# Sparse attention on one Trainium2 core: the masks move from TensorE to the maximum, the step pipeline gets one stage longer, and one weight load moves ahead of the parameters

## The reference

```
score = einsum(iw, relu(iq . ik)); causal keys only; idx = top_k(score, 128)
logits = q . k_sel * dh ** -0.5        # 8 heads of 128, 2 key/value heads
logits = where(valid, logits, -inf)
p = softmax(logits); o = p . v_sel
```

## Time and profile before

| | |
|---|---|
| median of 3 runs | 2177.53 us (2177.52 to 2177.66) |
| profiled execution | 2177.74 us |
| its span, first to last instruction | 2176.0 us |
| PE busy | 2135.4 us, 98% |
| DVE busy | 1285.1 us, 59% |
| ACT busy | 917.7 us, 42% |
| chain that ended last | PE 88%, DVE 5%, ACT 5% |
| the sparse attention (logits of step 0 to the first matmul of the next stage) | 1396.04 to 1467.43 us |

### The profile page before, as it was taken

How to read it: one execution, slowest core, us unless ns; L and a number is a source line. 1 busy time by engine, 2 the same in 40 slices (tenths; PEclk the granted TensorE clock), 3 DMA queues, 4 the chain that set the end, 5 groups by cost and what they waited for, 6 DMA issues and landing times.

```text
span 2176.0 us, 26697 instructions
## 1 busy us (share of the span) xinstructions
PE 2135.4 (98%) x10620; PEld 1730.3 (80%) x10620; DVE 1285.1 (59%) x1966; ACT 917.7 (42%) x1550; POOL 101.5 (5%) x155
## 2 busy tenths in 40 slices
PE   9999999999999999999999999999999999999998
PEld 7866688888888658888888878777788878888887
DVE  6446475555347767655543749456677657555634
ACT  4235553334325456333432642344445545333421
POOL 0000040000000003100000000000012200000000
PEclk9999999999999999999999999999999999999999
DMA  5312123333323203333332323202222023333332
GB/s 201 97 59 78 60 96 97 97 97 116 97 78 107 68 30 126 97 97 97 116 97 88 126 78 90 75 30 87 79 77 68 2 78 98 97 97 98 117 97 77
DMA packets 51099, 194.00 MB, mean 89 GB/s; under 512 B 5665, under 2 KB 5665, under 8 KB 49953
## 3 DMA queue, kind: packets, MB, share of 16 engines
q1 hardware_dynamic: 50976, 192.30, 28.1%
HBM read 188.09 MB, written 4.19 MB: 88 GB/s over the span
## 4 chain that ended last, share of the span: by engine, by line
PE 88%; DVE 5%; ACT 5%; issue 1%; DMA 1%; SPq 0%; ACTq 0%; DVEq 0%
PE bank L403 26%; PE bank L404 26%; PE bank L405 26%; PE bank L980 2%; PE bank L703 1%; DMA ring<-stream 1%; ACT arena L1265 1%; PE bank L681 1%; DVE small L1889 1%; ACT whi L1160 1%; PE bank L618 1%; DVE arena L2010 0%; DVE xs L1884 0%; PE bank L692 0%; PE bank L775 0%
## 5 line engine op out<-in xcount | busy, mean ns | idle before, releaser
L403 PE MATMUL bank<-xs,whi 128*128 128x512 f32 (+2 forms) x1992 | 770.8, 387 | 8.4 <-DVE xs L1884 2.9
L405 PE MATMUL bank<-xs,wlo 128*128 128x512 f32 (+2 forms) x1992 | 750.1, 377 | 0.0
L404 PE MATMUL bank<-xs,whi 128*128 128x512 f32 (+2 forms) x1992 | 749.9, 376 | 0.0
L1863 DVE TENSOR_TENSOR wlo<-ring,whi 128x1024 fp32r<-128x1024 f32 x333 | 415.2, 1248 | 294.8 <-ACT whi L1160 294.3
L1160 ACT ACTIVATE whi<-ring 128x1024 fp32r<-128x1024 f32 x333 | 350.4, 1054 | 262.4 <-DMA ring<-stream 262.2
L403 PEld LDWEIGHTS bank<-xs,whi 128*128 128x128 f32 x1992 | 375.4, 188 | 93.4 <-issue 12.2
L405 PEld LDWEIGHTS bank<-xs,wlo 128*128 128x128 f32 x1992 | 375.2, 188 | 69.0
L404 PEld LDWEIGHTS bank<-xs,whi 128*128 128x128 f32 x1992 | 375.8, 189 | 67.2 <-issue 2.9
L403 PE MATMUL bank<-whi,xs 128*128 128x512 f32 (+1 forms) x808 | 314.8, 390 | 1.6 <-issue 0.9
L405 PE MATMUL bank<-whi,xs 128*128 128x512 f32 (+1 forms) x808 | 311.7, 386 | 0.0
L404 PE MATMUL bank<-wlo,xs 128*128 128x512 f32 (+1 forms) x808 | 311.6, 386 | 0.0
(11 more groups left out here) (367 smaller groups left out, 1781.3 us busy)
## 6 DMA issues: line engine op xcount, KB each, us to landing
ring<-stream SPq DMA_DIRECT2D x333, 512.0 KB, 3.6
arena<-gains SPq DMA_DIRECT2D x5, 1024.0 KB, 5.8
arena<-xt SPq DMA_DIRECT2D x4, 512.0 KB, 6.1
arena<-xn SPq DMA_DIRECT2D x1, 2048.0 KB, 8.0
kept<-arena SPq DMA_DIRECT2D x1, 2048.0 KB, 7.2
arena<-kept SPq DMA_DIRECT2D x1, 2048.0 KB, 8.0
out<-arena SPq DMA_DIRECT2D x3, 512.0 KB, 2.6
con<-consts SPq DMA_DIRECT2D x1, 744.0 KB, 11.6
```

Source lines behind the costliest of these rows:

```text
L403: nc.tensor.matmul(out, ah, bh, start=first, stop=False)
L404: nc.tensor.matmul(out, ah, bl, start=False, stop=False)
L405: return nc.tensor.matmul(out, al, bh, start=False, stop=last)
L1863: V.tensor_tensor(wlo[:, v % SLOTS, :], ring[:, v % SLOTS, :], whi[:, v % SLOTS, :], ALU.subtract).then_inc(wlo_done, 1)
```

## The change

1. The mask matmuls on PE (line 683) are gone. DVE's maximum becomes one instruction that adds the mask to the logits, writes the negated sum back to the bank, and takes the minimum, which is the negated maximum; the minimum is read out by a second instruction. ACT's exponential gets scale -1. The wait for the masks moves from PE to DVE.
2. The pipeline is one step longer: after the logits of step n come the transposes of step n - 3 and the pv of step n - 4. ACT copies the transposed probabilities of step n - 3 ahead of the exponential of step n.
3. The three weight splits inside the stage are made at steps 5, 13 and 21 instead of 1, 9 and 17.
4. SP issues unit 1 ahead of the parameters.

The diff has the parts of SyncE, of the steps, of TensorE, of ScalarE and of VectorE in this order; the edit from `x == 1` to `x == 5` stands for ScalarE and for VectorE alike.

```diff
             for q in range(4):
                 sp.dma_start(U[:, 2 * q:2 * q + 2, :], xt[:, 2 * q:2 * q + 2, :]).then_inc(x_sem[q], 16)
+            sp.dma_start(ring[:, 1, :], stream[1]).then_inc(ring_sem[1], 16)
             sp.dma_start(par[:], params).then_inc(par_sem, 16)
-            for s in (1, 2, 3):
+            for s in (2, 3):
...
-                          more=[(idb[:], madd[:, i, 0:(i + 1) * P] if i else mqb[:], 0, (i + 1) * P)],
+                          mask=madd[:, i, 0:(i + 1) * P] if i else mqb[:],
...
-                for n in range(N + 3):
+                for n in range(N + 4):
...
-                        if n == 1:
-                            pe.wait_ge(vector_out, vector_at.find("masks"))
-                        nc.tensor.matmul(bank[b][:, 0:W], st["q"], st["k"], start=True, stop=False)
-                        for x, (l, r, c0, c1) in enumerate(st["more"]):
-                            m = nc.tensor.matmul(bank[b][:, c0:c1], l, r, start=False, stop=x == len(st["more"]) - 1)
-                        m.then_inc(tensor_out, tensor_at.next(name, "logits", n))
+                        nc.tensor.matmul(bank[b][:, 0:W], st["q"], st["k"], start=True, stop=True).then_inc(tensor_out, tensor_at.next(name, "logits", n))
...
-                    if 2 <= n < N + 2:
-                        k, st = n - 2, steps[n - 2]
+                    if 3 <= n < N + 3:
+                        k, st = n - 3, steps[n - 3]
...
-                    if n >= 3:
-                        k, st = n - 3, steps[n - 3]
+                    if n >= 4:
+                        k, st = n - 4, steps[n - 4]
...
+                    if 3 <= n < N + 3:
+                        k, st = n - 3, steps[n - 3]
+                        act.wait_ge(tensor_out, tensor_at.find(name, "t", k))
+                        if k >= 3:
+                            act.wait_ge(tensor_out, tensor_at.find(name, "pv", k - 3))
+                        A(st["ts"][:, 0:st["w"]], bank[5 + k % 2][:, 0:st["w"]], ACT.Copy).then_inc(scalar_out, scalar_at.next(name, "pt", k))
                     if n < N:
...
-                        A(st["ps"][:, 0:W], bank[st["lb"]][:, 0:W], ACT.Exp, bias=small[:, 200 + n % 4:201 + n % 4],
+                        A(st["ps"][:, 0:W], bank[st["lb"]][:, 0:W], ACT.Exp, bias=small[:, 200 + n % 4:201 + n % 4], scale=-1.0,
...
-                    if 2 <= n < N + 2:
-                        k, st = n - 2, steps[n - 2]
...
-                    if x == 1 and j < COUNT["z2b"]:
+                    if x == 5 and j < COUNT["z2b"]:
...
-                for n in range(N + 4):
+                for n in range(N + 5):
...
-                        V.tensor_reduce(small[:, 200 + n % 4:201 + n % 4], bank[steps[n]["lb"]][:, 0:steps[n]["w"]], AX_X, ALU.max, negate=True).then_inc(vector_out, vector_at.next(name, "max", n))
+                        logits, top = bank[steps[n]["lb"]][:, 0:steps[n]["w"]], small[:, 200 + n % 4:201 + n % 4]
+                        if name == "dsa":
+                            if n == 1:
+                                dve.wait_ge(vector_out, vector_at.find("masks"))
+                            V.tensor_tensor_reduce(logits, logits, steps[n]["mask"], -1.0, 3e38, ALU.add, ALU.min, top).then_inc(vector_out, vector_at.next(name, "max", n))
+                        else:
+                            V.tensor_reduce(top, logits, AX_X, ALU.max, negate=True).then_inc(vector_out, vector_at.next(name, "max", n))
```

More of the change, by code:

```diff
@@ L1297, in attention @@
                             act.wait_ge(tensor_out, tensor_at.find(name, "t", n - 4))
-                        A(st["ps"][:, 0:W], bank[st["lb"]][:, 0:W], ACT.Exp, bias=small[:, 200 + n % 4:201 + n % 4],
+                        A(st["ps"][:, 0:W], bank[st["lb"]][:, 0:W], ACT.Exp, bias=small[:, 200 + n % 4:201 + n % 4], scale=-1.0,
                                      accum_out=small[:, 204 + n % 4:205 + n % 4]).then_inc(scalar_out, scalar_at.next(name, "exp", n))
-                    if 2 <= n < N + 2:
-                        k, st = n - 2, steps[n - 2]
-                        act.wait_ge(tensor_out, tensor_at.find(name, "t", k))
-                        if k >= 3:
-                            act.wait_ge(tensor_out, tensor_at.find(name, "pv", k - 3))
-                        A(st["ts"][:, 0:st["w"]], bank[5 + k % 2][:, 0:st["w"]], ACT.Copy).then_inc(scalar_out, scalar_at.next(name, "pt", k))
                     if between is not None:
@@ L2016, in attention @@
                 N = len(steps)
-                for n in range(N + 4):
-                    if name == "dsa" and n >= 4 and steps[n - 4]["last"]:
-                        st = steps[n - 4]
-                        dve.wait_ge(tensor_out, tensor_at.find(name, "pv", n - 4))
+                for n in range(N + 5):
+                    if name == "dsa" and n >= 5 and steps[n - 5]["last"]:
+                        st = steps[n - 5]
+                        dve.wait_ge(tensor_out, tensor_at.find(name, "pv", n - 5))
                         V.tensor_tensor(MIX[:, st["dst"], :], MIX[:, st["dst"], :], bank[st["ob"]][:], ALU.mult).then_inc(vector_out, vector_at.next(name, "o", st["o"]))
```

## The result

| | before | changed |
|---|---|---|
| median of 4 runs, us | 2177.53 | 2162.98 |
| lowest and highest | 2177.06, 2177.66 | 2161.22, 2164.55 |
| profiled execution, us | 2177.74 | 2164.55 |
| its span, us | 2176.0 | 2162.8 |
| its mean granted clock | 0.995 | 0.996 |

The ratio is 0.9933, with a 95% interval of 0.9916 to 0.9951. The changed kernel is 14.5 us faster.

What follows compares the result with a forecast made beforehand. PE, busy 98% of the span, was taken as the bound. Masks 4.3, waits 5.85 and unit 1 1.15 us sum to 11.3 us saved, so 2166.2 us was forecast, range 2163.4 to 2170.5.

Steps and rivals of the forecast that it cites:

- Masks off PE: Sparse attention: removing 10240 columns of mask matmuls from PE saves 4.3 us, if PE remains the stage's bound.
- The maximum: Sparse attention, DVE: maximum with the mask takes 0.685 us at 512 columns, its read-out at most 0.154, covered by PE's work.
- The rival of the scan's rate: Sparse attention, DVE: new maximum takes 1.8 times as long, heads with splits lengthen, 2168 to 2169.7 us; 9 in 100.
- The waits: Sparse attention: of PE's 6.35 us of waits, the longer pipeline and later splits win 5.85 us.
- The rival that the waits stay: Sparse attention, ACT: exponential behind the copy gives back what the longer pipeline wins, 2172.1 us; 7 in 100.
- The splits: Sparse attention: moved four steps on, weight splits leave the empty pipeline at the beginning; price counted in the 6.35 us of waits.
- The 0.6 us to spare: Sparse attention, step 5: its probabilities are ready at 5.1 us behind DVE's split, PE wants them at about 5.7.
- Unit 1: Program start: issued ahead of the parameters, unit 1 lands earlier and PE gains 1.15 us, 1.3 at most.
- the rival that drew from it an even sharing: Program start: transfers run side by side, so unit 1 is not earlier, 2167.4 us; 13 in 100.
- The clock: Behind the sparse attention: PE's clock may fall elsewhere, half a 3.5 us stretch either way, 2164.5 to 2168 us; 5 in 100.

Runs made afterwards that it cites:

- pipeline alone: Kernel before with only the longer pipeline, the copy ahead of the exponential and the splits four steps on, masks left on PE; 2169.92 us, ratio 0.9966.
- unit 1 alone: Kernel before with only unit 1's transfer issued ahead of the parameters; 2174.23 us, ratio 0.9987.
- two delays: Kernel before with two or four constant matmuls (0.85 or 1.7 us) ahead of everything from the `mq` units on; 2178.30 and 2179.45 us.
- padded: Changed kernel with 24 constant matmuls (10.2 us) between the sparse attention and the next stage; 2174.05 us, ratio 0.9990.
- filled: Four constant matmuls put into PE's 2.23 us wait near 1548 us: kernel before 2173.28 us, changed kernel 2162.36 us.
- the control: Kernel before with four constant matmuls one product behind the 2.2 us wait near 1548 us, which stays empty; 2175.88 us, ratio 0.9998.

## Why the prediction was right, and where it was not

**Masks off PE: right.** 4.3 us predicted, 4.39 between pipeline alone and changed.

**The maximum: right.** 0.696 us at 512 for the predicted 0.685, the read-out 0.142 for at most 0.154. The rival of the scan's rate fell. The Trainium skill ("Vector Engine (DVE) Microarchitecture Reference", section "7. Points that are easy to get wrong") gives the halved throughput for one form, `S2S2D2_STT`, with two SBUF sources that are not bf16. The trace calls the new instruction CUSTOM_DVE_ANT_0 and doesn't show whether that rule covers it; no halving is seen, 0.696 us against 0.682 for the sum and 0.689 for the old maximum. Added up, DVE's groups in the stage rise from 41.5 to 46.4 us, by the 4.9 predicted, but its busy time in the window doesn't (38.20 before, 37.88 after): each read-out lies beside the end of the maximum and the reciprocal, as the changed kernel's timeline shows:

```profile
1398.55 0.69 DVE L2027 CUSTOM_DVE_ANT_0 bank<-bank,arena 128x512 f32<-128x512 f32 x1
...
1399.16 0.14 DVE L2027 DVE_READ_ACCUMULATOR2_ANT small<- 128x1 f32 x1
1399.16 0.16 DVE L2033 RECIPROCAL small<-small 128x1 f32<-128x1 f32 x1
```

**The waits: right.** 5.85 predicted, 5.70 measured by the pipeline alone, and 5.78 if the changed kernel's 10.08 are taken less the predicted 4.3. The stage was forecast at 61.2 and took 61.31, heads at 7.6 and took 7.57 to 7.58. The rival that the waits stay had named the wrong danger: it saw harm in the exponential behind the copy, and the old order showed that this order is needed for the gain. With the copy behind, the longer pipeline left the stage at 67.44, masks already gone. The prediction credited the longer pipeline alone; that was an error in the argument that the sum didn't show, since all three edits came together.

**The splits: right about the place, not about the size.** Only the first one costs, 2.02 us with the new pipeline. The 0.6 us to spare was far too small an estimate: 15.3 us of DVE instructions more in the stage cost 0.05 us.

**Unit 1: right.** 1.15 predicted, 1.34 to 1.38 between the two profiled executions above, 0.98 in the profile of unit 1 alone, and 1.0 at full clock in its runs. The start of unit 1 on PE varies from execution to execution: 13.67 to 14.54 us, on average 13.97, in the eight profiled kernels with the move, and 14.69 to 15.72, on average 15.13, in six without it, which makes 1.15 or 1.16. No wait for the later parameters shows. The Trainium skill ("DMA: Bandwidth & Descriptors", section "Two DMAs through the same engine are not ordered") promises no order across the 16 engines; the rival that drew from it an even sharing, worth 0, fell, since the transfer that was issued earlier was there earlier.

**The clock: this is the step that failed.** It stood among the rivals, worth up to 1.8 us either way and with 5 in 100, and counted nothing in the sum. The changed kernel's mean granted clock is 0.9973 where the kernel before has 0.9958. At 1.85 us per 0.001 that is 2.8 us, and with it the 11.3 us of the sum become 14.1, against 14.5 measured. At equal clock the gain is 11.1 to 11.5 us, so the rest of the sum stands; small errors in it, 0.1 us too little for the masks and 0.15 too much for the waits, cancel. The prediction looked at one stretch of 7 us; the sixteen profiled executions of this record have three to six stretches at the lower clock, the one at the end of the program included, and each can go or come, in the same kernel too.

**What makes the clock rise stays open.** It isn't the start time of what follows alone (two delays did nothing). The waits of the attention don't explain it alone (padded and unit 1 alone are equal within their error), though they have a part: the lower clock behind the wait that opens the old stage, in two of seven executions at 1.7 us each, comes to some 0.5 us on average, an estimate from few executions, and the change takes that wait away. It isn't only the one wait that I filled (the control rose too); but of the profiled executions where it is not filled, the clock fell there in seven of the nine with a longer stage and in none of the five with the stage at 61.3 or 61.4 us. Why is not shown. In the four kernels with the highest clock some later waits stand at other distances from the earlier ones than before, by added matmuls or by the attention's 10 us; but the same is true of the changed kernel without unit 1's move, which has 0.9964 with an error of 0.0005. No run here tells what counts. The two delays also leave open whether a shift of another size would do something.

No version tried beats the changed kernel: filled, it took 2162.36 us in 5 runs against 2162.68 in 10, which is no difference.

## What to carry to other kernels

Measure waits by the distance between the starts of a repeated block and a clean repeat of it (8 x 8.13 here): the busy share said 97%, the starts said 6.35 us of waits, and the forecast from it met the stage within about 0.1 us. Work taken off the bounding engine pays fully only when that engine no longer waits: the masks were worth 1.94 us with the waits and 4.39 without, so price both orders of a pair of edits. On an engine that works in order, put the instruction whose input is ready ahead of the one that waits for a long chain through another engine.

Ahead of a forecast to a few us in 2000, run the kernel before often enough to know how its time spreads with the granted clock, compare at equal clock, and put some 3 us for it into the range.

## What the runs showed of the hardware that I had not expected

- The add with a minimum in one instruction, which reads and writes PSUM, costs 296, 433, 563 and 696 ns at 128, 256, 384 and 512 columns, as much as a plain sum (682 at 512) and 4 to 9 ns more than the plain maximum of the same width (292, 424, 556 and 689). Its read-out of 142 ns begins before the main instruction has ended in the profile.
- One kernel's executions differ in their mean granted clock: 0.994 to 0.998 in 91 runs of the kernel before, which is 2179.7 to 2172.3 us.
- The same wait of PE, 2.23 us long, is followed by the lower clock in one kernel's execution and not in another's, and two executions of one kernel differ in the same way (0.57 and 1.00 from 1682 to 1686 us).
- A wait that is followed by the lower clock costs more than its length: 1.67 us more for the one of 1.69 us that opens the old stage.
- A kernel with four matmuls of no use was 4.3 us faster (0.9981, 0.9972 to 0.9991), all of it with the clock; why the clock rose is open.
